# Two of three two-pass experts moved among the light ones, and a light tile with an unsplit first down matrix

## What is computed

```python
def hier_moe(h, w_group, b_group, w_router, b_router, w_e_gate, w_e_up, w_e_down):
    ...
    e_w, e_idx = lax.top_k(jax.nn.softmax(e_logits, axis=-1), TOP_K)
    e_w = e_w / e_w.sum(axis=-1, keepdims=True)
    ids = g_top[:, None] * EXPERTS_PER_GROUP + e_idx
    ...
    for e in range(N_EXPERTS):
        a = jax.nn.silu(hf @ w_e_gate[e]) * (hf @ w_e_up[e])
        out = out + gates[:, e:e + 1].astype(hf.dtype) * (a @ w_e_down[e])
```

## Time and profile before

| | |
|---|---|
| median of three runs | 1677.28 us (1676.32 to 1678.29) |
| profiled execution, its own time | 1676.23 us |
| its span | 1674.6 us |
| instructions | 27905 |
| TensorE busy | 1626.1 us (97%) |
| VectorE busy | 1325.7 us (79%) |
| ScalarE busy | 1035.5 us (62%) |
| GpSimd busy | 81.1 us (5%) |
| mean over the span | 235 GB/s |

### The profile page before, as it was taken

One profiled execution on the slowest core, in us unless ns is written; L12 is line 12 of the kernel. 1 busy time (PEld: TensorE's weight loads), 2 busy tenths in 40 slices (PEclk: granted clock), 3 DMA queues, 4 the chain that ended last, 5 costly groups with the idle time before them and its releaser, 6 DMA issues.

```text
span 1674.6 us, 27905 instructions
## 1 busy us (share of the span) xinstructions
PE 1626.1 (97%) x10552; PEld 1426.8 (85%) x10552; DVE 1325.7 (79%) x1514; ACT 1035.5 (62%) x1153; POOL 81.1 (5%) x94
## 2 busy tenths in 40 slices
PE   7999999999999999999998989999999999999998
PEld 7999999888887677777767978999999999998887
DVE  6577878855799999999986897687767879687776
ACT  5355765645789999999986464454344394453443
POOL 0000000000000000000006210000000020000000
PEclk9999999999999999999998999999999999999999
DMA  9643344366899999999998434446554565445650
GB/s 323 209 140 102 102 151 130 134 252 214 302 415 418 422 422 423 422 422 423 422 412 282 145 126 137 140 152 221 180 188 153 162 201 177 128 163 177 199 175 25
DMA packets 186667, 393.24 MB, mean 235 GB/s; under 512 B 6992, under 2 KB 151120, under 8 KB 162000
## 3 DMA queue, kind: packets, MB, share of 16 engines
q1 hardware_dynamic: 181600, 374.32, 61.1%
q0 software_dynamic: 4976, 17.67, 2.8%
HBM read 381.34 MB, written 10.62 MB: 234 GB/s over the span
## 4 chain that ended last, share of the span: by engine, by line
PE 65%; DVE 14%; DMA 10%; ACT 5%; issue 5%; POOL 0%; SPq 0%; DVEq 0%; ACTq 0%; POOLq 0%
PE ps L956 9%; DMA raw<-w_e_up_dram 8%; DVE wlo L2411 7%; PE ps L1142 6%; PE ps L962 5%; PE ps L669 4%; PE ps L674 4%; PE ps L670 4%; PE ps L971 4%; PE ps L1091 3%; PE ps L1097 3%; PE ps L1093 2%; ACT whi L1686 2%; PE ps L687 1%; PE ps L688 1%
## 5 line engine op out<-in xcount | busy, mean ns | idle before, releaser
L2411 DVE TENSOR_TENSOR wlo<-raw,whi 128x2048 fp32r<-128x2048 f32 (+2 forms) x358 | 810.5, 2278 | 138.3 <-ACT whi L1686 131.2
L1686 ACT ACTIVATE whi<-raw 128x2048 fp32r<-128x2048 f32 (+2 forms) x358 | 675.3, 1890 | 298.1 <-PE ps L962 113.7
L1091 PE MATMUL ps<-whi,xh 128*128 128x512 f32 x528 | 160.3, 396 | 0.0
L956 PE MATMUL ps<-xb,whi 128*128 128x512 f32 x672 | 160.2, 391 | 0.0
L669 PE MATMUL ps<-xh,whi 128*128 128x256 f32 x608 | 151.7, 289 | 4.6 <-DVE arena L2493 2.6
L670 PE MATMUL ps<-xl,whi 128*128 128x256 f32 x608 | 149.0, 285 | 0.0
L956 PEld LDWEIGHTS ps<-xb,whi 128*128 128x128 f32 x672 | 124.1, 188 | 24.3
L1097 PE MATMUL ps<-wlo,xh 128*128 128x512 f32 x528 | 143.3, 396 | 1.4 <-DVE wlo L2411 1.4
L669 PEld LDWEIGHTS ps<-xh,whi 128*128 128x128 f32 x608 | 117.7, 194 | 6.0 <-DVE arena L2493 3.0
L1097 PEld LDWEIGHTS ps<-wlo,xh 128*128 128x128 f32 x528 | 97.2, 188 | 29.5 <-DVE wlo L2411 9.6
L670 PEld LDWEIGHTS ps<-xl,whi 128*128 128x128 f32 x608 | 117.9, 194 | 0.3
(11 more groups left out here) (509 smaller groups left out, 3184.5 us busy)
## 6 DMA issues: line engine op xcount, KB each, us to landing
raw<-w_e_gate_dram SPq DMA_DIRECT2D x64, 1024.0 KB, 10.1
raw<-w_e_up_dram SPq DMA_DIRECT2D x64, 1024.0 KB, 10.3
raw<-w_e_down_dram SPq DMA_DIRECT2D x64, 1024.0 KB, 10.3
raw<-ffn_w_gate_up_dram SPq DMA_DIRECT2D x44, 1024.0 KB, 5.1
raw<-w_in_dram SPq DMA_DIRECT2D x30, 1024.0 KB, 5.9
raw<-ffn_w_down_dram SPq DMA_DIRECT2D x22, 1024.0 KB, 4.9
raw<-xa_w_kv_dram SPq DMA_DIRECT2D x16, 1024.0 KB, 5.5
raw<-xa_w_q_dram SPq DMA_DIRECT2D x8, 1024.0 KB, 5.1
```

The lines of the kernel that those rows point to most:

```text
L956: nc.tensor.matmul(ps[:, bank + b, :], wh[:, k, b * P:b * P + P], xb[:, k, :, :].rearrange("p a t -> p (a t)"), start=k == 0, stop=False, ...
L1091: nc.tensor.matmul(o, h[:, k, :], wh[:, k, :], start=part == 0 and k == 0, stop=False)
L1686: nc.scalar.activation(whi[u % HL][:, 0:n], raw[u % RAW][:, 0:n], ACT.Copy).then_inc(hi_ready, 1)
L2411: v.tensor_tensor(wlo[u % HL][:, 0:n], raw[u % RAW][:, 0:n], whi[u % HL][:, 0:n].bitcast(F32), ALU.subtract).then_inc(lo_ready, 1)
```

## The change

The order of tiles is no longer that of ranks. `ORDER` is rank 0, ranks 3 to 14, rank 1, ranks 15 to 22, rank 2, ranks 23 to 31, so tile 13 and tile 22 are the two-pass tiles of ranks 1 and 2, each between light ones. Since a store in another order would overwrite rows, the results of ranks 1 and 2 go aside, to 512 rows ahead of the others in a longer `compact_y`; `rows_i` gets a computed shift for pairs of these ranks, and two new DRAM copies put finite values into those rows ahead of the stage.

A light tile changes in three ways. Its first down half is no longer split: no `hi` and `lo` for that unit, four plain float32 matmuls straight from `raw` against unsplit hidden features (`hid_whole`), and the load of six units on waits until TensorE has used it. The halves are summed ahead of the turn: ScalarE copies the lower 64 rows of gate and up, VectorE adds the upper 64 rows from PSUM (`halves_added`), ScalarE takes SiLU, VectorE multiplies (`hidden_summed`), and TensorE's turn is four transposes. And all hardware loops over tiles are unrolled.

Loops in `hi`, `lo` and the waits of the dense layers stay as they are. In the diff, cut to its core:

```diff
+ORDER = (0, *range(TWICE, FEW), 1, *range(FEW, FEW + 8), 2, *range(FEW + 8, TILES))
+ASIDE = {1: 0, 2: 1}
...
+def starts_of(rank):
+    return (2 * rank, 2 * rank + 1) if rank < TWICE else (rank + TWICE,)
...
+def light(m):
+    return ORDER[m] >= HEAVY
+FIRST = [sum(len(starts_of(r)) for r in ORDER[:m]) for m in range(TILES + 1)]
...
+        whole = {moe + 6 * (m + 1) + 2 if m < TILES - 1 else moe + 6 * TILES - 2 for m in range(TILES) if light(m)}
+        def parts_to(u):
+            return u + 1 - sum(w <= u for w in whole)
+        def last_in(u):
+            return next((w for w in range(u - HL, -1, -HL) if w not in whole), None)
...
                 if i is not None:
-                    sp.wait_ge(lo_ready, i * step + (u - RAW + 1))
+                    sp.wait_ge(lo_ready, i * step + parts_to(u - RAW))
+                elif u - RAW in whole:
+                    sp.wait_ge(unit_used, u - RAW + 1)
                 elif u >= RAW:
-                    sp.wait_ge(lo_ready, u - RAW + 1)
+                    sp.wait_ge(lo_ready, parts_to(u - RAW))
...
+                for m in range(1, TILES):
+                    u, before, e = p0 + 6 * m - 2, e, expert(m)
+                    load(u, wg[0][e])
+                    load(u + 1, wu[0][e])
+                    load(u + 2, wg[1][e])
+                    load(u + 3, wu[1][e])
+                    load(u + 4, wdn[0][before])
+                    load(u + 5, wdn[1][before])
...
+                def turn_hidden(m):
+                    first, w = FIRST[m], SLOTS if light(m) else P
+                    pe.wait_ge(r_hid, passes(m)[-1] + 1)
                     if first >= 1:
-                        pe.wait_ge(r_hid_l, add + first)
-                    if 1 <= m <= TWICE:
+                        pe.wait_ge(r_hid_l, first)
+                    if m >= 1 and light(m - 1):
+                        pe.wait_ge(r_hid_whole, sum(light(a) for a in range(m)))
+                    if m >= 1 and twice(m - 1):
...
+                            mm = nc.tensor.transpose(ps[:, 6 + s - first, k * w:k * w + w],
+                                                     features(hid[s % 2][0:w, :], k), ident[0:w, 0:w])
...
+                def down_whole(u, m):
+                    s = FIRST[m]
+                    pe.wait_ge(raw_landed[u % RAW], 16 * (u // RAW + (u % RAW > 0)))
+                    pe.wait_ge(r_hid_whole, sum(light(a) for a in range(m + 1)))
+                    pe.wait_ge(r_y, s)
+                    weights = wview_raw(u, 2, D)
+                    for n in range(2):
+                        for k in range(2):
+                            mm = nc.tensor.matmul(ps[0:SLOTS, 4 + n, :], hid_whole[s % 2][:, k, :],
+                                                  weights[:, k, 512 * n:512 * n + 512], start=k == 0, stop=False)
+                    mm.then_inc(unit_used, 1)
...
+                    rows_by(hid_l, wh)
+                    low_in(u)
+                    rows_by(hid_h, wl, stop=half == 1).then_inc(unit_used, 1)
...
+                def gate_out(u, s):
+                    act.wait_ge(unit_used, u)
+                    act.wait_ge(r_hid, s - 1)
+                    nc.scalar.activation(sil[s % 2][0:SLOTS, :], ps[SLOTS:P, s % 2, :], ACT.Copy).then_inc(pair_out, 1)
+                def up_out(u, s):
+                    act.wait_ge(unit_used, u)
+                    act.wait_ge(r_hid_mm, s - 1)
+                    nc.scalar.activation(hid[s % 2][0:SLOTS, :], ps[SLOTS:P, 2 + s % 2, :], ACT.Copy).then_inc(pair_out, 1)
+                def silu_summed(m):
+                    act.wait_ge(gate_summed, sum(light(a) for a in range(m + 1)))
+                    gate = sil[FIRST[m] % 2][0:SLOTS, :]
+                    nc.scalar.activation(gate, gate, ACT.Silu).then_inc(r_silu, 1)
...
+                        turned = ps[:, 6, 0:256].rearrange("p (k s) -> p k s", k=4)
+                        act.wait_ge(r_hid_mm, first + 1)
+                        nc.scalar.activation(hid_whole[first % 2], turned[:, 0:2, :], ACT.Copy).then_inc(r_hid_whole, 1)
+                        nc.scalar.activation(hid_h[first % 2][:, 2:4, 0:SLOTS], turned[:, 2:4, :],
                                              ACT.Copy).then_inc(r_hid_h, 1)
...
+                    for a in ahead[:1]:
+                        act.wait_ge(unit_used, u - 2)
+                        window(a, m + 1)
+                    if not light(m):
+                        if m >= 2:
+                            y_there(u, m - 2)
+                        hi(u + 2)
+                        hi(u + 3)
+                        hi(u + 4)
+                        hidden_high(m - 1)
+                        hi(u + 5)
+                        silu(u + 3, s)
+                        hi(u + 6)
                     else:
-                        silu(u + 3, s)
-                    hi(u + 6, i, 6 * LOOP)
-                    if light:
-                        up_out(u + 4, s, i)
-                    if more:
-                        hi(u + 7, i, 6 * LOOP)
+                        hi(u + 2)
+                        hi(u + 3)
+                        hi(u + 4)
+                        if twice(m - 2):
+                            y_there(u, m - 2)
+                        hidden_high(m - 1)
+                        if not twice(m - 2):
+                            y_there(u, m - 2)
+                        hi(u + 5)
+                        gate_out(u + 3, s)
+                        up_out(u + 4, s)
+                        hi(u + 6)
+                        silu_summed(m)
...
+                def halves_added(m):
+                    s, n = FIRST[m], sum(light(a) for a in range(m))
+                    gate, up = sil[s % 2][0:SLOTS, :], hid[s % 2][0:SLOTS, :]
+                    dve.wait_ge(pair_out, 2 * n + 1)
+                    v.tensor_tensor(gate, ps[0:SLOTS, s % 2, :], gate, ALU.add).then_inc(gate_summed, 1)
+                    dve.wait_ge(pair_out, 2 * n + 2)
+                    link(v.tensor_tensor(up, ps[0:SLOTS, 2 + s % 2, :], up, ALU.add))
+                def hidden_summed(m):
+                    s = FIRST[m]
+                    gate, up = sil[s % 2][0:SLOTS, :], hid[s % 2][0:SLOTS, :]
+                    dve.wait_ge(r_silu, s + 1)
+                    v.tensor_tensor(up, up, gate, ALU.mult).then_inc(r_hid, 1)
...
+                    lo(u + 2)
+                    lo(u + 3)
+                    lo(u + 4)
+                    hidden_low(m - 1)
+                    if light(m):
+                        for a in ahead[:1]:
+                            dve.wait_ge(unit_used, u - 2)
+                            window(a, m + 1)
+                        lo(u + 5)
+                        halves_added(m)
+                        lo(u + 6)
+                        hidden_summed(m)
...
+            v.tensor_scalar(aside_by[:, 0:1], aside_at[:, 0:1], -1.0, -2.0 * T, ALU.mult, ALU.add)
+            link(v.tensor_tensor(aside_by[:, 1:2], aside_at[:, 0:1], aside_at[:, 1:2], ALU.subtract))
+            v.tensor_scalar(aside_by[:, 1:2], aside_by[:, 1:2], float(T), None, ALU.add)
+            v.tensor_scalar(aside_by[:, 2:3], aside_at[:, 1:2], float(T), None, ALU.add)
+            link(v.tensor_scalar(moved, rows_f, 2.0 * T, None, ALU.add))
+            for a in range(3):
+                link(v.tensor_scalar(shift, rows_f, aside_at[:, a:a + 1], aside_by[:, a:a + 1], ALU.is_ge, ALU.mult))
+                link(v.tensor_tensor(moved, moved, shift, ALU.add))
+            v.tensor_copy(rows_i, moved)
...
+            for a in range(2):
+                pool.dma_start(compact[(2 + a) * T:(3 + a) * T, :],
+                               t["xT"].rearrange("(a b) n -> a (b n)", b=DC // 2)).then_inc(y_stored, 16)
...
+                for s, aside in zip(passes(m), range(2)):
+                    if ORDER[m] in ASIDE:
+                        at = T * ASIDE[ORDER[m]] + P * aside
+                        rows = compact[at:at + P, :]
+                    else:
+                        at = START_AT[s]
+                        row = pool.value_load(start_i[0:1, at:at + 1], min_val=0, max_val=PAIRS_OUT)
+                        rows = compact[2 * T:, :][bass.ds(row, rows_of(m)), :]
+                    pool.wait_ge(r_y, s + 1)
                     pool.sem_inc(store_go, 1)
-                pool.dma_start(compact[bass.ds(row, n), :], y_out[s % 2][0:n, :]).then_inc(y_stored, 16)
+                    pool.wait_ge(y_stored, 16 * (s + 2))
+                    pool.sem_inc(store_go, 1)
+                    pool.dma_start(rows, y_out[s % 2][0:rows_of(m), :]).then_inc(y_stored, 16)
```

More of the change, by code:

```diff
@@ L1892, in tile_twice @@
                     ahead = passes(m + 1)
-                    row = [row_start(s) for s in ahead]
                     hi(u + 2)
@@ L1902, in tile_twice, with tile @@
                     hi(u + 5)
-                    act.wait_ge(first_done, m + 1)
-                    window(ahead[0], m + 1, row[0])
```

(20 more changed lines are left out.)

342 lines of the change are left out of this document (128 added, 214 removed).

## The result

In shared runs the changed kernel took 1691.93 us (median of four, 1688.87 to 1693.15), the kernel before 1677.54 (1676.32 to 1678.29): ratio 1.009, 95% interval 1.0078 to 1.0102. The forecast of 1676.5, and the range up to 1686, were wrong: the change costs 14.4 us. The profiled executions have spans of 1674.6 and 1689.5 us, 14.9 apart.

What follows compares the result with a forecast made beforehand. Light tiles were taken as bound by transfers, two-pass tiles by TensorE. Stage -2.7, start +1.7, code +0.7 and tail -0.4 summed to -0.7 us: median 1676.5, range 1664 to 1686.

Steps and rivals of the forecast that it cites:

- TensorE's terms per unit: Matmul time of one expert unit on TensorE: 1.82 us light, 2.72 for 128 rows, 5.44 for two passes.
- the eight light tiles without help: Light tiles following the 128-row ones: 122.1 us as before, since DMA ends last and a faster tile changes nothing.
- both two-pass tiles: The two-pass tiles moved between light ones: 28.6 us each.
- the two waits behind each of them: TensorE idle behind a moved two-pass tile: 1.8 us ahead of the two-pass down, 3.8 ahead of the next turn.
- 3.8 us of idle TensorE: Second light tile behind a moved two-pass tile: the turn waits for ScalarE's result copies; bounds 0 and 4.
- the held load: Load of six units on, waiting until the unsplit matrix is used: issued 15 us after that tile's start.
- the light floor: Light tile's time when engines, not transfers, set it: 14.2 us after the change, bounds 13.9 and 14.8.
- The start: Ahead of the stage, eleven tiny VectorE operations precede the gathered columns: +1.7 us, bounds 0 and 2.6.
- The first (the bank works, 12 us better): Stage: result-copy wait and held buffer don't hurt, each moved tile saves about 6 us more: 1664.5; chance 0.22.
- The second rival: Light tiles: hand-offs between ScalarE and VectorE replace transfers as the bound, 0.5 us longer per tile: 1688; chance 0.22.
- The third (light tiles not bound by transfers): Light tiles all run at 14.2 us, 23 us off in all: 1653; chance 0.03.
- a gain of 2.7: Expert stage from the start of tile 1: 521.3 us after the change against 524.0 before.

Runs made afterwards that it cites:

- nat_order: The changed kernel with tiles in their natural order, so the new light tile alone: 1678.36 us, ratio 1.0018 to the kernel before.
- best: Changed kernel, result copies ahead of high halves, hidden values ahead of the next split, rows-aside VectorE block behind hidden(1): 1675.39 us, ratio 0.9996 to before.
- half-loaded kernels: Natural-order kernel with new light tile, and kernel before, each loading half of every expert unit from the second tile on: 1660.39 and 1664.03 us.
- fill_idle: The changed kernel with 16 extra unread matmuls ahead of the turn's wait for the result copies: 1685.04 us, ratio 1.006 to before.
- y_first: The changed kernel with ScalarE's two result copies of a two-pass tile ahead of the three high halves: 1682.26 us, ratio 1.0037 to before.
- y_split: Changed kernel, result copies ahead of high halves, first down matrix split again in light tiles right behind two-pass ones: 1683.83 us, ratio 1.0051 to before.

## Why the prediction was wrong

**Right.** TensorE's terms per unit, the 128-row tiles, the eight light tiles without help, both two-pass tiles, and the two waits behind each of them: their places, their releasers and nearly their lengths (2.00 for 1.8, 4.12 for 3.8). The unsplit down took 3.58 us to the start of the next matmul (617.62 to 621.20) where 3.46 was forecast, within the bounds of 2.72 and 3.78:

```profile
617.62 3.65 PE L1163 MATMUL ps<-raw,scr 128*64 128x512 f32 x8
```

That is eight records for four matmuls. The four passes of the Trainium skill's FP8 and Floating Point Precision, TensorE Precision Notes, had given an estimate of 3.63; the trace agrees to 0.05.

**Wrong, first step: what a wait of TensorE costs.** "3.8 us of idle TensorE" was entered as 3.8 us. It cost 4.1 and then 2.3 more, at the lower clock, and this lay on the way to the unsplit down, whose use releases the next load. The run with filled waits shows the clock's share of it, 4.8 us at the two places. The second moved tile paid once more: its 2.0 us wait for hidden_low was followed by the lower clock too, which makes the tile behind it 23.2 instead of 21.6.

```profile
754.00:758.00 4.00, 3.71 (x9) 2.94 (x10) 3.96 (x6) 3.85 (x5) 0.17 (x1) 0.57 0.97 398
```

**Wrong, second step: the tiles behind the held load.** Seven were put at 104.7, from a load that starts 15 us after the tile, lands 4.9 later and is followed by a unit every 2.48 us, the 33rd being used 3.5 after its landing. They took 111.7. The load started after 18.1, so 3.1 of the 7.0 come by the forecast's own working (2.3 of the clock, 0.3 of the longer wait, the rest of the turn and the unsplit down). It landed 4.7 after its issue, 0.2 better. The 33rd, issued at 700.12, landed 9.75 later, at 709.9: 83.9 us for 32 units and their stores, where the forecast has 81.3, so 2.6 more. And TensorE began with it 5.0 after that and not 3.5, which is 1.5 more. DMA was full all the while, as forecast:

```profile
620.00:625.00 5.00, 5.00 (x20) 2.69 (x19) 4.96 (x6) 4.50 (x5) 0.00 (x0) 1.00 0.51 190
625.00:630.00 5.00, 5.00 (x24) 3.93 (x23) 5.00 (x3) 4.35 (x5) 0.00 (x0) 1.00 1.01 421
626.00:710.00 84.00, 83.28 (x312) 49.86 (x313) 74.07 (x56) 70.81 (x68) 3.75 (x6) 1.00 1.01 420
```

In the last window 35.27 MB were moved, some 1.0 more than 32 units with their stores and code: bytes of the loads that stood behind the 33rd. A sum that lets each unit land before the next one begins misses this. So the transfers were not slower than forecast; they started late, and the unit that was waited for shared them.

**Wrong, third step: the light floor,** 14.2 on paper and 14.6 on the chip, and the floor of before, 14.8 rather than 14.6. What is gained behind a moved tile before transfers catch up is 15.2 less the floor per tile; at 14.6 that is 0.6 and not 1.0. The forecast's 102.9 for TensorE alone would be 3.8 + 7 x 14.6 = 106.0 with it, above the 104.7 that was taken; so this step alone makes the seven at least 1.3 longer.

**The start.** +1.7 forecast. The gathered copy came 2.25 later in the profiled pair, and 1.3 by the means of all traces (328.9 against 327.6 of the two with the kernel before's code there), both within the bounds of 0 and 2.6. How much of that reaches the end stayed open. For unrolling, 0.3 MB of code had been estimated; the instruction queue shows 0.13 MB more (1.16 against 1.03), and no run separates what it costs.

**Missed entirely:** the load of memT, which comes earlier because the windows of a light tile are taken earlier in it. The forecast counted its 2 us for the tile, but not that it moves ahead of the last units. Issuing it later gave 2.0 to 3.6 us. How much of that the change itself had lost is less clear: the last interval between turns is 0.9 longer in nat_order and best than in the kernel before, and 1.3 to 1.5 shorter with the later load.

**The rivals.** The first (the bank works, 12 us better) was refuted as the kernel stood, and half true of what it could be: without the waits and with memT later, the stage takes 521.7 us from the start of tile 1 (354.5 to 876.2), against 524.0 before. By chance, that is the forecast's own 521.3, reached by a kernel without the waits that the forecast had charged. The second rival named 1688, not far from 1691.9, and for the wrong reason: the light tile isn't slower for its hand-offs, as nat_order and the half-loaded kernels show (14.6 against 14.8 without the bound of transfers). The number alone would have looked like a confirmation. The third (light tiles not bound by transfers) was refuted by nat_order: DMA at 1.01.

**The forecast's logic.** It listed the right waits and then found a gain of 2.7, since it let the bank pay for them. Each moved tile shifts its surplus of TensorE work behind transfers that were to run ahead; but six raw buffers hold only so much. DMA rests at 0.47 through the moved tile even in the best version:

```profile
560.00:580.00 20.00, 20.00 (x82) 13.79 (x81) 8.21 (x8) 7.66 (x7) 0.00 (x0) 1.00 0.47 186
```

and only two tiles behind it run faster than the 15.2 of light tiles with a 32-row store (14.6 twice, then 15.2, between the turns at 617.6 and 661.9). So the whole prize was 1.4 to 2.1 us per moved tile (half of 2.8 and of 4.3), and one wait of 4 us with its clock, at each, was enough to turn it over.

## What to carry to other kernels

When an order of work is changed, look for in-order queues whose written order still fits the old neighbours: here ScalarE's result copies behind two roundings, and VectorE's hidden values behind one remainder. Moving a few lines gave back all of the 14 us. A wait of TensorE of some 4 us is to be priced twice, for its length (4.1 here) and for the slower clock after it (2.3 here); and a buffer that is freed by the waiting engine passes both on to the transfers. When a trigger is tied to a step (a load behind "the last windows"), ask where that step goes when the tile around it changes its shape.

## What the runs showed of the hardware

- The granted clock fell to 0.50 behind each of the two waits of 4.1 us, and the first sixteen matmuls behind it took 2.3 us longer; with 3.8 us of matmuls in the wait it stayed at 1.00. Waits of 2.0 us were followed by it in one of two places in the changed kernel (0.57 from 754 to 758) and in fill_idle (0.76 from 751 to 758), and in neither of the two in y_first and y_split. What decides there stays open.
- Plain float32 with 512 columns: eight records in 3.65 us for four matmuls, 0.9 us each (3.58 to the next start), four times the 0.227 of a rounded operand.
- Small VectorE operations take 0.14 to 0.29 us each, but one of them takes up to 1.03 us, and it isn't the same one: before, it was L3130; in the changed kernel it is one of the new block, 0.77 for four elements per partition; in nat_order another, 1.02 for a single element. What they share is GpSimd's second cast, the one that writes `xc_l`. In all fourteen traces the long operation is the one that runs while this cast ends, and it ends within 0.03 us of it; it is a TENSOR_SCALAR in eight and a TENSOR_TENSOR in six of them. Here it ends at 326.93, and the cast at 326.91. So the cost goes with GpSimd's cast, and not with the operation that meets it.

```profile
326.16 0.77 DVE L3184 TENSOR_SCALAR arena<-arena 128x4 f32<-128x4 f32 x1
```

```profile
325.86 1.05 POOL L3528 CAST xc_l<-arena 128x1024 fp32r<-128x1024 f32 x1
```
